# Moving the splits of two weight tiles at the beginning of layer 1 in a three-model fp32 transformer kernel

## The reference, cut to what matters

```python
a_lat = rms_norm(h, norm1_g[l]) * (1 + sc1) + sh1
a_ctx = rms_norm(hc, norm1_g[l]) * (1 + modc[1]) + modc[0]
# odd mixer: projections of both, then two kinds of attention
p_lat = h_lat @ w_in                  # cq, dq (queries) and ck, cv, dk, dv
p_ctx = h_ctx @ w_in[:, OD_Q:]        # keys and values alone
cq = apply_rope(rms_norm(split_heads(cq), cq_g))      # 8 heads of 64
dq = apply_rope(rms_norm(diff_split(dq), dq_g))       # 4 heads of 2 x 64
ck = apply_rope(rms_norm(split_heads(ck), ck_g)); dk = likewise
y = merge(window_gqa(cq, ck, cv, sink), diff_attention(dq, dk, dv, lam))
```

## Time and profile before

| | |
|---|---|
| median of 3 runs | 1960.55 us (1958.65 to 1961.99) |
| the profiled execution, its own time | 1962.71 us |
| its span, first to last instruction | 1960.8 us |
| PE busy | 1764.6 us (90%) |
| DVE busy | 1251.0 us (64%) |
| ACT busy | 824.9 us (42%) |
| mean granted TensorE clock | 0.933 of full speed |

### The profile page before, as it was taken

The page is one execution under the profiler, slowest core; times in us unless marked ns, Lnnn a source line. Parts: engine busy times, 40 slices in busy tenths (PEclk is TensorE's granted clock), DMA queues, the critical chain, the costliest instruction groups (busy, mean ns, idle before and its releaser), DMA issues. The chain is left out here.

```text
span 1960.8 us, 22044 instructions
## 1 busy us (share of the span) xinstructions
PE 1764.6 (90%) x8958; PEld 1480.0 (75%) x8958; DVE 1251.0 (64%) x1709; ACT 824.9 (42%) x999; POOL 134.4 (7%) x128
## 2 busy tenths in 40 slices
PE   4897998899799997799779999999988988889998
PEld 1774786788677886788667888888868856768987
DVE  5355685467645553575648888898886545565644
ACT  5322232422112223333326776777744433535542
POOL 1230000200020011230010000000030000000000
PEclk8896997999999998889779999999998979898999
DMA  7431332255544541211047888888855521135553
GB/s 289 110 108 65 129 130 88 84 194 178 182 187 173 201 148 67 96 52 55 11 150 272 320 319 321 316 326 326 329 207 173 190 67 52 65 129 183 174 193 128
DMA packets 61437, 332.59 MB, mean 170 GB/s; under 512 B 16836, under 2 KB 17411, under 8 KB 28178
## 3 DMA queue, kind: packets, MB, share of 16 engines
q1 hardware_dynamic: 56080, 321.54, 45.4%
q10 hardware_dynamic: 4354, 6.32, 1.0%
q0 software_dynamic: 896, 3.26, 0.5%
HBM read 329.96 MB, written 1.13 MB: 169 GB/s over the span
## 5 line engine op out<-in xcount | busy, mean ns | idle before, releaser
L1957 DVE TENSOR_TENSOR wlo__65<-raw__64,whi__66 128x2048 fp32r<-128x2048 f32 (+2 forms) x68 | 157.0, 2309 | 117.0 <-ACT whi__66 L1443 117.0
L1957 DVE TENSOR_TENSOR wlo__61<-raw__60,whi__62 128x2048 fp32r<-128x2048 f32 (+3 forms) x56 | 125.4, 2239 | 83.6 <-ACT whi__62 L1443 83.6
L1443 ACT ACTIVATE whi__66<-raw__64 128x2048 fp32r<-128x2048 f32 (+2 forms) x68 | 127.1, 1869 | 122.7 <-DMA raw__64<-in_ffn_w 49.8
L1957 DVE TENSOR_TENSOR wlo__69<-raw__68,whi__70 128x2048 fp32r<-128x2048 f32 (+4 forms) x52 | 110.2, 2118 | 42.8 <-ACT whi__70 L1443 42.7
L1443 ACT ACTIVATE whi__62<-raw__60 128x2048 fp32r<-128x2048 f32 (+3 forms) x56 | 102.9, 1837 | 73.5 <-DMA raw__60<-in_ev_w_in 22.1
L1443 ACT ACTIVATE whi__70<-raw__68 128x2048 fp32r<-128x2048 f32 (+4 forms) x52 | 90.4, 1739 | 30.3 <-DMA raw__68<-in_w_ff 11.1
L1990 DVE SCALAR_TENSOR_TENSOR wsum__71<-raw__68,silu_rows 128x1024 f32<-128x1024 f32 x84 | 99.9, 1220 | 3.5 <-DMA raw__68<-in_ada_w 3.0
L2953 POOL TENSOR_TENSOR keep__58<-keep__58,keep__59 128x1 f32<-128x1 f32 (+3 forms) x48 | 49.2, 1027 | 632.3 <-DVE keep__58 L2029 632.3
L2212 DVE TENSOR_REDUCE keep__58<-ps 128x1 f32<-128x256 f32 (+1 forms) x104 | 56.6, 544 | 27.7 <-PE ps L891 20.9
L1443 ACT ACTIVATE whi__139<-raw__137 128x2048 fp32r<-128x2048 f32 (+2 forms) x15 | 26.2, 1744 | 108.9 <-DMA raw__137<-in_ffn_w 108.9
L1957 DVE TENSOR_TENSOR wlo__138<-raw__137,whi__139 128x2048 fp32r<-128x2048 f32 (+2 forms) x15 | 31.2, 2079 | 55.2 <-ACT whi__139 L1443 55.2
(11 more groups left out here) (1095 smaller groups left out, 5446.9 us busy)
## 6 DMA issues: line engine op xcount, KB each, us to landing
raw__68<-in_ada_w SPq DMA_DIRECT2D x26, 1024.0 KB, 5.0
raw__64<-in_moe_w SPq DMA_DIRECT2D x24, 1024.0 KB, 6.3
raw__60<-in_moe_w SPq DMA_DIRECT2D x24, 1024.0 KB, 6.6
raw__68<-in_moe_w SPq DMA_DIRECT2D x16, 1024.0 KB, 5.8
raw__226<-in_moe_w SPq DMA_DIRECT2D x16, 1024.0 KB, 5.1
raw__230<-in_moe_w SPq DMA_DIRECT2D x16, 1024.0 KB, 6.1
raw__60<-in_ada_w SPq DMA_DIRECT2D x15, 1024.0 KB, 6.1
raw__64<-in_ffn_w SPq DMA_DIRECT2D x13, 1024.0 KB, 5.0
```

Source lines behind the costliest of these rows:

```text
L1443: e.activation(t.hi(), t.raw(), ACT.Copy).then_inc(*did("hi", i))
L1957: e.tensor_tensor(t.lo(), t.raw(), t.hi().bitcast(F32), ALU.subtract).then_inc(*did("lo", i))
```

## The change

Only the values of `ahead` change, at four places (two in ScalarE's program, two in VectorE's; `norm_by_token` serves two norms, and only layer 1's `o` is touched). No instruction is added or removed. From the end of the feed-forward stage on, `ahead` stays 1 through the second norm, so that at `("nt", "o", 1, 0)` the bound is 103 and tile 103 isn't split there. It becomes 2 for the feeds of the four `ckv` products (`n` = 103, bound 105), so that tiles 103 and 104 are both split there: on ScalarE behind the two squares of `cq`, on VectorE behind the rotation of the second `cq`, and on both ahead of the turned queries' parts. It is 1 again from there on, and tile 105 is split at the first turned keys as before, alone.

```diff
@@ scalar: norm_by_token
             norm_turned(N, 0)
-            at["ahead"] = 2
+            at["ahead"] = 1 if N == "o" else 2
             norm_square(N, 3)
@@ scalar: behind the squares of cq
-        at["ahead"] = 1
+        at["ahead"] = 2
         for t in range(4):
             feed(("prod", "od", "ckv", t))
+        at["ahead"] = 1
         for t in range(2):
             odd_hi("cq", t, CQ3, 4)
```

## The result

The changed kernel takes 1952.71 us (median of 10 executions, 1947.7 to 1956.44), the kernel before on the same chips 1960.68 us (10 executions, 1956.96 to 1961.99): ratio 0.9961, 95% interval 0.9949 to 0.9972. It is 8.0 us faster (by the interval 5.5 to 10.0). Forecast were 7.1 us, that is 1953.4 us, in a range of 1950.5 to 1958.0.

What follows compares the result with a forecast made beforehand. TensorE's stops of 7.1 us (tile 104) and 4.0 us (second norm) traced to VectorE's queue: 2.0 us later at the key tiles' chain, 2.2 back, plus 6.85 idle gives 7.1 us, 1960.55 to 1953.4; range 1950.5 to 1958.0.

Steps and rivals of the forecast that it cites:

- Tile 103 away from the norm: Second norm: first eviction 1.6 us earlier, 0.4 lost in ScalarE's queue, so the chain to the second rotation 1.2 us earlier.
- Both splits behind the rotation: Behind the second rotation: ScalarE's high parts cost nothing, VectorE's low parts 2.2 us each; turned queries' low parts 2.0 us later.
- The turned keys: Turned keys: only tile 105's low part remains ahead; VectorE done 0.2 us earlier, its 6.85 us idle time there gone.
- the lead: Turned keys: ScalarE's four high parts end at about 823, about 1 us ahead of VectorE's 823.9.
- The new wait of TensorE: Behind the turned queries: TensorE waits 1.5 us for tile 103's low part, ready only at 809.5.
- The join: Turned keys' low parts start at 823.9 instead of 831.00, 7.1 us earlier; tile 105's first step at 828.7.
- Behind the join: Rest of the kernel: same instructions in the same order, nothing at a fixed time, so the 7.1 us reach the end.
- the clock eats part of it: Rival: the new wait drops the clock under the dq products, 0.5 to 1.7 us lost, 1953.9 to 1955.1; chance 0.20.
- Given back in the attention: Rival: behind 842 us one more low-clock spell costs about 7 us, time 1960.4, no difference; chance 0.10.
- slower: Rival: the attention's low-clock mechanism twice as large, two more spells give 1967.5; chance 0.05.
- the spell at 930 us: Attention, 930 to 944: 14 us at mean clock 0.52 behind waits of about 1 us, said to cost about 7 us.
- The wait that changes its name: Rival: VectorE's own chain becomes the bound; a stop of 4 to 7 us gives 1957 to 1960; chance 0.05.

Runs made afterwards that it cites:

- the second profile: The changed kernel run and profiled once more, nothing altered, against the kernel before: ratio 0.9957 (0.9943 to 0.9971), stage 38.70 us.
- the halves: Against the kernel before: only tile 103 away from the second norm, ratio 0.9993; only tile 104 split ahead of the turned queries, 1950.14 us, ratio 0.9944.
- The pair of runs: Tile 104 ahead alone plus one VectorE product before dq 0's scaling: two SBUF operands, stage 39.22 us; one operand in PSUM, 38.06; one execution each.
- the last kernel: Tile 104 ahead alone, plus dq 0's square and mean ahead of the turned keys' parts and tile 105's low part behind: 1949.78 us, ratio 0.9945.
- the kernel with tile 105 late: Tile 104 ahead alone, plus tile 105's low part on VectorE moved behind the turned keys' low parts and dq 0's mean: stage 37.65 us, ratio 0.9939.

## Why the prediction was right

1. *Tile 103 away from the norm, 1.2 us.* The last low part came 791.69 - 786.27 = 5.42 us behind the load's issue, before 796.49 - 789.76 = 6.73: 1.3 us. The first eviction came 1.6 us earlier, so 0.3 us were lost in between, forecast 0.4: VectorE's first low part waits 1.01 us at 788.72 for the high part, 0.70 before.
2. *Both splits behind the rotation.* 803.53 and 805.74, pitch 2.21 us, as forecast; ScalarE's two cost nothing (793.44 to 797.2, then 6.70 us idle). The turned queries' low parts came 21.67 us behind the issue, before 19.85: 1.8 us later, forecast 2.0.
3. *The turned keys.* VectorE was through with tile 105 at about 820.2 and had no idle time. ScalarE's high parts were over at 818.7: a lead of 1.5 us, forecast 1. But the lead was mis-measured: VectorE takes the four high parts one by one and needs only the first to start. By the start of the high parts the lead was 2.8 us (817.37 to 820.18), and 0.9 us in the second profile; where VectorE waits, in the kernel before, the distance is 0.42.
4. *The new wait of TensorE.* 1.58 us, forecast 1.5.
5. *The join.* 33.91 us behind the issue, before 831.00 - 789.76 = 41.24: 7.33 us, forecast 7.1.
6. *Behind the join* nothing was given back: the second profile of the changed kernel took 1125.3 us there, those of before 1125.0 and 1125.1.

The rivals: *the clock eats part of it* did not happen in the first profile, where the two `dq` products ran at 1.00. In the second its condition came true and its price did not: the clock fell to 0.50 under the products, TensorE was 1.9 us later at the turned keys, and the stage was the same 38.70 us. The prediction took the lead for 1 us and so let 0.5 to 1.7 us of the gain go; the lead was longer. The prediction weighed here what the Trainium skill says (TensorE: Matmul & The Clock Gate, "A second HAM failure mode: psum-queue depth-cycling"), that short idles between groups of products make the clock swing and cost throughput. The traces agree that it swings, but not with every idle: of the changed kernel's two profiles the stop of 2.64 us was followed by 0.50 in one and by 1.00 in the other, the one of 1.6 us the reverse. The length of the idle alone didn't decide. What it cost TensorE did not reach the time, as VectorE was the later one. *Given back in the attention* and *slower* did not happen either. (The waits of about 1 us ahead of the spell at 930 us do not stand in the earlier trace rows; the trace has them, 0.82 us at 929.08 and 1.05 at 932.17.) *The wait that changes its name* did in part: 3.56 us of TensorE's time before the first scores are now a wait for VectorE's queue (1.83 in the second profile), 1.36 before. A wait of about 3 us was in the forecast, but its "again" misreads the trace of before, which has 1.36.

How much of the good number is luck: the stage's 7.33 us against 7.1 isn't, since every link of the sum came out within 0.3 us but for the lead. That the median moved by 8.0 us, 0.7 more than the stage, lies within its interval; and half of the 15 us by which the first profiled execution was shorter is chance.

What the prediction left undone lies in its own terms. In its sum the splits cost 2.2 us each, the norm gives 1.2 and the idle time ahead of the turned queries takes up 1.2. So tile 103 moved alone is worth next to nothing (0.2 us), and on top of tile 104 it costs 1.0: tile 104 alone gives more than both. The prediction didn't say so; the halves measured it, 0.3 to 0.8 us for the first and 1.1 us lost for the second.

## What to carry to other kernels

Cost a moved instruction on the queue that sets the next join, not on the one that waits now: here a move that saved 1.3 us at a wait put 2.2 us into that queue and ate 1.1 us of the other move's gain. When a join passes from one engine to another, try each half of the edit alone. And before you put an instruction with two SBUF operands into idle time of VectorE, look whether that idle time is a wait for POOL: here the instruction started first and POOL's result came 2 us later.

## What the runs showed of the hardware that I had not expected

POOL's root of 128x8 takes 1.63 us alone or beside a VectorE instruction that reads one operand from PSUM, and 3.60 to 3.61 us if a VectorE product or difference with two SBUF operands (2.28 us) started just before it: the extra is 1.97 us, nearly the rest of VectorE's instruction. The Trainium skill states this (SBUF — State Buffer, "Who interferes with whom" and "Summary: rules for kernel authors"): a VectorE instruction with two SBUF inputs excludes a GpSimd instruction that reads SBUF, and whichever is second waits for the whole of the first. The pair of runs agrees with it where POOL is second. The other order stands elsewhere in the kernel before:

```profile
95.76 4.60 POOL L2985 TENSOR_TENSOR in__84<-in__84,keep__49 128x2048 f32<-128x2048 f32 x1
96.43 6.07 DVE L1957 TENSOR_TENSOR wlo__65<-raw__64,whi__66 128x2048 fp32r<-128x2048 f32 x1
```

VectorE's low part, 2.28 us in this stage, takes 6.07 and ends 2.1 us behind POOL's product, which agrees too. One case doesn't: in the last kernel tile 105's low part (819.32) started 0.5 us before POOL's root ended (818.16 and 1.63) and still took 2.28 us. So the end of that root did not hold VectorE up.

The kernel's executions differ by more than the stage's change would let one see in one profile: the same program took 1120.8 and 1125.3 us for the same rest, and the difference is TensorE's busy time at a different granted clock. And a stop of TensorE isn't followed by the lower clock each time: behind the first stop of this stage it fell to 0.50 after 2.64 us (changed kernel, first profile), and stayed at 1.00 after 2.64 us (second profile) and after 3.84 us (the kernel with tile 105 late).
